# Early loads and an eleventh weight buffer for the experts, and their rows fetched one expert at a time

## What is computed

```
logits = h @ router                      # 256 x 8
top_logit, top_e = top_k(logits, 2)
gate = softmax(top_logit)
for expert e, over the rows routed to it:
    y = (silu(rows @ wg[e]) * (rows @ wu[e])) @ wd[e]     # wg, wu: 1024 x 3584, wd: 3584 x 1024
out = sum of the two gated y of each token
```

## Time and profile before

| | us |
|---|---|
| median of 3 runs | 2739.91 (2738.45 to 2746.37) |
| the profiled execution | 2743.33 |
| its span in the trace | 2741.4 |
| PE busy | 2639.1 (96%) |
| VectorE busy | 1197.7 (44%) |
| ScalarE busy | 442.7 (16%) |
| GpSimd (POOL) busy | 108.2 (4%) |

### The profile page before, as it was taken

The page is one execution under the profiler, slowest core; times in us unless marked ns, Lnnn a source line. Parts: engine busy times, 40 slices in busy tenths (PEclk is TensorE's granted clock), DMA queues, the critical chain, the costliest instruction groups (busy, mean ns, idle before and its releaser), DMA issues.

```text
span 2741.4 us, 48517 instructions
## 1 busy us (share of the span) xinstructions
PE 2639.1 (96%) x20537; PEld 1656.5 (60%) x20537; DVE 1197.7 (44%) x2895; ACT 442.7 (16%) x1054; POOL 108.2 (4%) x154
## 2 busy tenths in 40 slices
PE   8899999989899999999999998999979999999998
PEld 7659984865333233232332386699458967876993
DVE  3855675474110110110110166467655665344675
ACT  1231000133011010110110113200041001132000
POOL 1000000000100000000000011000000000050001
PEclk9999999999999999999999999999999999999999
DMA  7556555855999999999999946245504554232552
GB/s 224 175 182 206 169 170 183 269 167 197 338 418 419 417 416 411 410 419 406 408 420 410 413 153 108 70 154 170 172 14 154 170 172 135 77 85 70 169 170 93
DMA packets 234112, 642.91 MB, mean 235 GB/s; under 512 B 15673, under 2 KB 149185, under 8 KB 203056
## 3 DMA queue, kind: packets, MB, share of 16 engines
q1 hardware_dynamic: 225968, 616.89, 60.8%
q0 software_dynamic: 7264, 21.56, 3.5%
q10 hardware_dynamic: 672, 1.41, 0.1%
HBM read 626.73 MB, written 13.08 MB: 233 GB/s over the span
## 4 chain that ended last, share of the span: by engine, by line
PE 89%; DVE 6%; DMA 2%; issue 1%; POOL 1%; ACT 0%; DVEq 0%; ACTq 0%; POOLq 0%
PE pacc L1194 14%; PE pacc L1268 10%; PE pt L961 10%; PE pacc L1285 7%; PE pt L1268 7%; PE pt L1194 6%; PE pacc L1232 6%; PE pada L1294 4%; PE po L1268 3%; PE pacc L1135 3%; PE pt L1232 3%; PE pt L1173 2%; PE pt L1680 2%; PE pacc L1115 2%; PE po L1232 1%; DVE prob L2187 1%
## 5 line engine op out<-in xcount | busy, mean ns | idle before, releaser
L2527 DVE TENSOR_TENSOR gateb<-kT,pt 128x512 f32<-128x512 f32 (+1 forms) x32 | 19.9, 621 | 534.5 <-PE pt L1268 533.8
L1268 PE MATMUL pacc<-ring,bigc 128*32 128x512 f32 (+1 forms) x1920 | 188.3, 550 | 1.1 <-DVEq L2518 1.1
L961 PE MATMUL pt<-ring,hT 128*128 128x256 f32 x832 | 184.4, 381 | 0.0
L961 PEld LDWEIGHTS pt<-ring,hT 128*128 128x128 f32 x832 | 156.9, 190 | 25.6 <-issue 5.2
L1194 PE MATMUL pacc<-probT,prob 128*128 128x128 f32 x1440 | 170.6, 275 | 0.0
L1194 PEld LDWEIGHTS pacc<-probT,prob 128*128 128x128 f32 x1440 | 165.6, 192 | 0.0
L1285 PE MATMUL pacc<-ring,bigc 128*32 128x512 f32 x1280 | 151.2, 592 | 0.0
L1268 PE MATMUL pt<-ring,bigc 128*32 128x512 f32 (+1 forms) x1280 | 140.7, 560 | 8.2 <-DMA ring<-in_moe_w_up 8.2
L1232 PE MATMUL pacc<-prob,chunks 128*128 128x512 f32 x282 | 136.4, 592 | 0.0
L1268 PEld LDWEIGHTS pacc<-ring,bigc 128*32 128x32 f32 x1920 | 58.8, 110 | 127.2 <-issue 124.9
L2313 DVE TENSOR_TENSOR prob<-ring 128x512 f32<-128x512 f32 x86 | 59.5, 692 | 154.8 <-PE pacc L1194 108.5
(11 more groups left out here) (463 smaller groups left out, 4280.9 us busy)
## 6 DMA issues: line engine op xcount, KB each, us to landing
ring<-in_moe_w_down SPq DMA_DIRECT2D x80, 1024.0 KB, 17.5
ring<-in_w_gate_up SPq DMA_DIRECT2D x66, 1024.0 KB, 5.1
ring<-in_w_ada SPq DMA_DIRECT2D x48, 1024.0 KB, 5.3
ring<-in_moe_w_gate SPq DMA_DIRECT2D x48, 1024.0 KB, 8.5
ring<-in_moe_w_up SPq DMA_DIRECT2D x48, 1024.0 KB, 19.5
ring<-in_w_down SPq DMA_DIRECT2D x33, 1024.0 KB, 4.9
ring<-in_moe_w_gate SPq DMA_DIRECT2D x32, 768.0 KB, 15.0
ring<-in_moe_w_up SPq DMA_DIRECT2D x32, 768.0 KB, 12.8
```

What stands on the lines that cost most here:

```text
L961: ins = pe.matmul(t[:, q * 256:q * 256 + n], src[:, k, q * P:q * P + P], w[:, k, 0:n], start=(k == 0), stop=(k == KC - 1))
L1268: ins = pe.matmul(into[32 * j:32 * j + 32, 0:w].rearrange("p (t n) -> p t n", n=2 * 32), hcurv[:, kc, 32 * g:32 * g + 32], strip_columns(t ...
```

## The change

Three edits go together.

- `MOE_SLOTS` goes from 10 to 11; the eleventh buffer is columns 4096 to 6144 of `big`. The places are dealt anew: tile m with m % 11 = i below 6 goes to ring buffer (`pre_moe` + i - 2) % 6, the others to `xc`, the two halves of `prob`, `biasb` and the new one.
- Tiles 6, 9 and 10 of expert 0 are loaded by SP between the last `w_out` tile and the last six `w_ada` tiles. The other tiles of expert 0 below 11 are then loaded in the order 2, 3, 7, 4, 0, 1, 5, 8, and from tile 11 on, and for the experts 1 to 7, in order of m as before.
- POOL fetches the rows of one expert at a time from `slot_rows` straight into `next_slots`: those of expert 1 after the scatter, those of e + 2 when the sums of expert e are handed over. The copy on VectorE goes away with the array in `big`.

Semaphores are merged (`picked` into `routed`, `slots_arranged` and `y_shifted` into `rows_turned`), and the dense branch, which no longer has that part of `big`, uses other columns and waits for the fetches at its end.

```diff
-MOE_SLOTS = 10
+MOE_SLOTS = 11
+MOE_EARLY = (6, 9, 10)
+MOE_FIRST = (2, 3, 7, 4, 0, 1, 5, 8)
...
             i = m % MOE_SLOTS
-            return (pre_moe + i) % SLOTS if i < SLOTS else i
+            return (pre_moe + i - 2) % SLOTS if i < SLOTS else (6, 8, 9, 7, 10)[i - SLOTS]
...
-                   [xc[:, :], biasb[:, :], prob[:, 0:2048], prob[:, 2048:4096]]
+                   [xc[:, :], biasb[:, :], prob[:, 0:2048], prob[:, 2048:4096], big[:, 4096:6144]]
...
+            def load_expert(e, m, early=False):
...
+                i = moe_place(m)
+                if not early:
+                    sp.wait_ge(slot_free[i], e * moe_uses[i] + (m // MOE_SLOTS + 1))
+                sp.dma_start(moe_view(tile), src).then_inc(tile_loaded[i], 16)
...
                     load(n, item[1], item[2])
                     n += 1
+                    if n == pre_moe - MODS_ROUTER:
+                        sp.wait_ge(conv_taken, 2)
+                        sp.wait_ge(conv_ready, 2)
+                        for m in MOE_EARLY:
+                            load_expert(0, m, early=True)
...
-                    with sp.Fori(0, NE) as e:
-                        for m, tile in enumerate(moe_tiles):
...
+                    for m in MOE_FIRST + tuple(range(MOE_SLOTS, len(moe_tiles))):
+                        load_expert(0, m)
+                    with sp.Fori(1, NE) as e:
+                        for m in range(len(moe_tiles)):
+                            load_expert(e, m)
...
             pool.sem_inc(slot_free[7], 1)
+            pool.sem_inc(slot_free[10], 1)
...
-            for j in range(STRIPS):
-                pool.dma_start(slots_in[32 * j:32 * j + 32, 1:NE, :].rearrange("p e (g n) -> p (e g) n", g=3),
-                               slot_rows[CAP:NE * CAP, 256 * j:256 * j + 256].rearrange("(g t) n -> t g n", t=32))\
-                    .then_inc(slots_loaded, 16)
+
+            def fetch_slots(e):
+
+                for j in range(STRIPS):
+                    pool.dma_start(next_slots[32 * j:32 * j + 32, :].rearrange("p (g n) -> p g n", g=3),
+                                   slot_rows[e * CAP:e * CAP + CAP, 256 * j:256 * j + 256]
+                                   .rearrange("(g t) n -> t g n", t=32)).then_inc(slots_loaded, 16)
+
+            fetch_slots(1)
...
                     pool.dma_start(expert_rows[o + 32 * g:o + 32 * g + 32, 512:1024],
                                    ysum[64 * (g - 1):64 * (g - 1) + 32, 1, :]).then_inc(y_written, 16)
+                if e + 2 < NE:
+                    fetch_slots(e + 2)
                 pool.wait_ge(y_written, 64 * (e + 1))
                 pool.sem_inc(y_free, 1)
...
-                        ve.wait_ge(slots_loaded, 16 * STRIPS)
-                        ve.tensor_copy(next_slots, big[:, bass.ds((e + 1) * EW, EW)]).then_inc(slots_arranged, 1)
-                        ve.wait_ge(slots_arranged, e * 2 + 1)
+                        ve.wait_ge(slots_loaded, e * (16 * STRIPS) + 16 * STRIPS)
                         arrange(next_slots)
-                        weigh(e * 2 + 2)
-                    add_rest(e)
+                        weigh(e * 3 + 1)
+                    add_rest(e, last)
```

More of the change, by code:

```diff
@@ L333, in build @@
         y_copied = sem("y_copied")
-        y_shifted = sem("y_shifted")
         y_ready = sem("y_ready")
@@ L747, in load @@
                 sp.dma_start(slot_view(n, kind), src).then_inc(tile_loaded[n % SLOTS], 16)
+            gate_rows_of = W["moe_w_gate"][0].rearrange("e k f -> (e k) f")
+            up_rows_of = W["moe_w_up"][0].rearrange("e k f -> (e k) f")
+            down_rows_of = W["moe_w_down"][0].rearrange("e f n -> (e f) n")
+            def load_expert(e, m, early=False):
+                tile = moe_tiles[m]
+                kind, half, c, _ = tile
+                if kind == "d":
+                    src = down_rows_of[bass.ds(e * FF1 + 2 * P * c, 2 * P), :].rearrange("(p k) n -> p k n", k=2)
+                else:
+                    f0 = HALVES[half][0]
+                    src = (gate_rows_of if kind == "g" else up_rows_of)[bass.ds(e * D + P * c, P), f0:f0 + moe_width(tile)]
+                i = moe_place(m)
+                if not early:
+                    sp.wait_ge(slot_free[i], e * moe_uses[i] + (m // MOE_SLOTS + 1))
+                sp.dma_start(moe_view(tile), src).then_inc(tile_loaded[i], 16)
             for item in stream:
@@ L1308, in moe_sparse @@
             def moe_sparse():
-                pe.wait_ge(picked, 1)
+                pe.wait_ge(routed, 2)
                 for half in range(2):
@@ L2505, in arrange @@
                     ve.transpose(hcur.rearrange("p (b g t) -> p g b t", b=KC, t=32),
-                                 slots.rearrange("p (g b i) -> p g b i", b=KC, i=32)).then_inc(slots_arranged, 1)
+                                 slots.rearrange("p (g b i) -> p g b i", b=KC, i=32)).then_inc(rows_turned, 1)
                 def weigh(n):
-                    ve.wait_ge(slots_arranged, n)
+                    ve.wait_ge(rows_turned, n)
                     ve.tensor_tensor(hcurv, hcurv, free(g[:, 0:1], [[1, KC], [0, CAP]]), ALU.mult).then_inc(h_current, 1)
@@ L2536, in turn, with add_rest @@
                                  product[:, k % 2, 0:w].rearrange("p (t n k) -> p t k n", n=32, k=2)).then_inc(turned_taken, 1)
-                def add_rest(e):
+                def add_rest(e, last):
                     ve.wait_ge(y_done, e * 2 + 2)
@@ L2542, in add_rest @@
                     for g in range(2):
-                        ve.tensor_copy(yside[64 * g:64 * g + 32, :], down_rest[64 * g + 32:64 * g + 64, :]).then_inc(y_shifted, 1)
-                    ve.wait_ge(y_shifted, e * 2 + 2)
+                        ve.tensor_copy(yside[64 * g:64 * g + 32, :], down_rest[64 * g + 32:64 * g + 64, :]).then_inc(rows_turned, 1)
+                    ve.wait_ge(rows_turned, e * 3 + (2 if last else 3))
                     ve.tensor_tensor(ysum[0:96, 1, :], down_rest[0:96, :], yside[0:96, :], ALU.add).then_inc(y_ready, 1)
@@ L2630, in moe_dense @@
                 settle()
+                ve.wait_ge(slots_loaded, 16 * STRIPS * (NE - 1))
             def already(q):
@@ L2978, in _ @@
                         go(ve.tensor_scalar(pick[:, q, :], pick[:, q, :], den[:, 2 + q:3 + q], None, ALU.mult))
-                    tell(picked)
+                    tell(routed)
                     find_rows()
```

18 lines of the change are left out of this document (2 added, 16 removed).

## The result

The changed kernel takes 2812.99 us (median of 5 runs, 2809.25 to 2814.4), the kernel before 2738.45 (5 runs, 2734.53 to 2746.37): ratio 1.0266, 95% interval 1.0254 to 1.0279. Slower by 74.5 us, where 53.5 was forecast: 2793 us, in a range of 2768 to 2822. Run again on another chip it took 2809.78 against 2741.34, ratio 1.0245 (1.0228 to 1.0263). The profiled execution took 2812.99 us for a span of 2811.2.

The account below looks back on a forecast made before the run. PE was taken as the bound (busy 96% of the span), the DMA queues close behind; 49.3 + 16.2 + 1.5 - 13.5 = +53.5 us, giving 2796.8 for the profiled execution, 2793 for the median, range 2768 to 2822.

Parts of the forecast that it names:

- its rivals (2806 to 2835): Slower outcomes: clock falling at every boundary 0.14, thin queue with later landings 0.09, expert 0 keeping its stall 0.05.
- SP waits with tile 0 until tile 44 is used: Seven expert boundaries: tile 0 issued at E - 2.18, E being the next expert's stall-free start, after some 26 us idle.
- Tile 0 lands late by 3.1 us: Each boundary: tile 0, loaded into an empty queue, lands after 5.3 us, so PE stalls 3.1 us.
- Tile 1 stalls for 3.9 us: Each boundary: tile 1 is issued 1.2 us after tile 0's start, lands at E + 9.6, and stalls PE 3.9 us.
- Tiles 2 to 10 follow without a stall: Each boundary: these tiles land 2.50 us apart and are used at 2.58, so no more stall, but no lead.
- the first term of the sum: Landing stalls for tiles 0 and 1: 7.0 us per boundary, 49.3 us for seven.
- The six fetches cost 16.2 in full: Row fetches just after the boundaries of experts 0 to 5 delay weights 2.7 us each, 16.2 us; low end nothing.
- Rival: the clock on top, 20.3: PE's clock falls after the stalls at every boundary, 7 x 2.9 = 20.3 us more, about 2814; chance 0.14.
- Expert 0 saves 13.5: Expert 0's stall and slow clock both go, -13.5 us; either half alone leaves at most a 3 us stall.
- The end, +1.5: End of the experts' stage: the context load into `xc` lands later against the end, +1.5 us (-1 to +3).
- Before the stage, nothing: Three early tiles loaded before the w_ada tiles cost nothing, PE's need being covered by 20 us and more.
- 3 us to spare per expert: Per expert the queues need 105.1 us for weights and PE 108.2, so PE sets the pace with 3 us spare.

Follow-up runs that it names:

- the version without the fetches: The changed kernel without the row fetches of experts 2 to 7, which compute with expert 1's rows: 2801.41 us, ratio 1.0231 to the kernel before.
- the fillers: The changed kernel plus matmuls on a constant at the seven boundaries, three before the wait for tile 0, four before tile 1: 2803.05 us, ratio 1.0237.
- The rows alone: The kernel before with only the row fetches made one expert at a time, no early tiles, ten buffers: 2744.8 us, ratio 1.0014.
- the two early tiles alone: The kernel before with only tiles 6 and 7 of expert 0 loaded early, ten buffers, one big row fetch: 2732.85 us, ratio 0.9979.
- the version with both changes: The changed kernel with filler matmuls before tiles 0 and 1 and without the row fetches of experts 2 to 7: 2793.06 us, ratio 1.0201.
- the spread dealing: The changed kernel, eleven buffers, none reused within nine tiles, early tiles 0, 5, 11: 2735.11 us; also without row fetches of experts 2 to 7: 2729.34 us.

## Why the prediction was right

The mechanism came as forecast, and 2812.99 us is in the range. But it is 20 us above the 2793 of the sum, in the band that the prediction gave to its rivals (2806 to 2835), and two errors in the sum work against each other. By its steps:

- *SP waits with tile 0 until tile 44 is used.* Right: issued at E - 2.38 (forecast E - 2.18), after a gap of 25.9 us (some 26), with 0 GB/s before it.
- *Tile 0 lands late by 3.1 us.* Right: 3.05 to 3.33. A tile issued into the empty queue was in use after 818.50 - 813.00 = 5.5 us; the forecast had 5.3. The formula that the prediction quotes from the Trainium skill (DMA: Bandwidth & Descriptors, Anatomy of one DMA) is given there for DMAs issued by GpSimd; its 4.4 us for a tile of SP's is 1.1 under this row.
- *Tile 1 stalls for 3.9 us.* Right where the clock is full during tile 0: at the second boundary of the version without the fetches it was issued 1.19 us after tile 0's start (forecast 1.2; 932.38 against 931.19) and in use 5.0 later, a stall of 3.6. In the change the first one is issued at 820.56, 2.06 behind the start, at a slow clock, and in use 6.3 later, beside the rows; over the seven boundaries the pause is 3.1 to 4.4. The waits sum to 49.3 us, the very number of the forecast, but partly by luck: they are not the whole price.
- *Tiles 2 to 10 follow without a stall.* Wrong, and with it the first term of the sum was too small. Without the fetches the boundaries cost 71.0 us, not 49.3. Of the 21.7 us more, the fillers take away 11.5: that is slow clock, which the forecast left to a rival. The other 10.2 stay at full clock, where a boundary costs 59.5 / 7 = 8.5 us, not 7.0: at the second one, from start to start, 3.4 for tile 0, 3.8 for tile 1, and 0.5 and 1.1 for small pauses at tiles 2 and 8. At each of the seven, two tiles land 3.2 to 4.0 us apart where the others land 2.5 apart, and each time a 16 KB packet of the instruction queue lies between the two landings or 1 us before (the lines stand below the list); in the stage such a packet comes every 8 to 24 us; whether it is the cause was not tested.
- *The six fetches cost 16.2 in full.* Too large. Taking them out of the change saves 5.0 us at the boundaries. The 16.3 of the versions with fillers is no confirmation of the price of 2.7: it is 1.9 each at the four boundaries with the clock held, and 4.2 each at the two where it was not. The landing times give 1.5. The Trainium skill (DMA: Bandwidth & Descriptors, Issuing engines are not separate DMA queues) says that transfers of all issuing engines interleave on the same 16 DMA engines; the traces agree: with POOL's fetch SP's tile 1 came 7.82 us behind tile 0 at the second boundary with fillers, without it 6.35.
- *Rival: the clock on top, 20.3.* The fall itself came as described, 0.50 behind tile 1, but its price is smaller. Without the fetches it is 11.5, or 1.6 a boundary, where 2.9 was said. With them it is 0.9 at each of the four boundaries where the fillers held the clock, and the fillers' loss at the first and sixth leaves 0.2 in all. So that the time came out at this rival's 2814 is luck. The Trainium skill (TensorE: Matmul & The Clock Gate, HAM oscillation) advises to arrange the loop so that the engine is not left cold by waits for DMA; here the clock fell as it says, and fillers that held it at 1.00 at five of seven boundaries moved the stage by 1.0 us in 943.
- *Expert 0 saves 13.5.* 13.3. (Of the 5.3 us that the prediction puts to the clock there, its two slow tiles show 1.9 and 2.9.) The rows alone do all of it, the two early tiles alone 5.8 of it (115.86); a stall of 3.0 and one of 2.6 remained there, where 3 at most was said for either half.
- *The end, +1.5.* +2.3.
- *Before the stage, nothing.* +6.3 and +6.9 in the two profiles of the change; not foreseen, and the cause is open, as above.

The packets of the weights (q1) and the one of the instruction queue (q8) from 1063 to 1065 us in the version with both changes, between two landings at 1062.05 and 1066.08:

```profile
q1 hardware_dynamic: 115, 0.82, 98.5%
q8 instruction: 1, 0.02, 3.2%
```

In sum, 2796.8 was forecast for the profiled execution, and the difference to 2812.99 is 10.5 (boundaries: 21.7 too little for the tiles, 11.2 too much for the fetches) + 6.3 (before the stage) + 0.8 (end) + 0.2 (expert 0) - 1.6 (the rest) = 16.2 us.

One more step was wrong and did not show in the sum: "3 us to spare per expert". It took the 419 GB/s of a single window of 62 us for the rate of the whole stage. The kernel before gains at most 1.1 us per expert, and the spread dealing without the fetches none. By the forecast's numbers the change with harmless dealing would have given 2726. It gives 2740.49 with ten buffers and 2735.11 with eleven: what expert 0 wins by the smaller fetches, the later experts pay back.

## What to carry to other kernels

When N tiles go round M buffers and the issuer takes them in order, look at the seam: at N mod M = 2 the first tile of the next round waits for the last but one of this round, and all prefetch is gone, though there is one buffer more; deal the buffers by distance of reuse and check the seam tile by tile. Filling the queue with other tiles first makes it worse, since the urgent one then lands behind them. And where the queue's share is 1.0, its GB/s do not tell whether it has time to spare, since they may be the consumer's pace: follow the landing time of one tile from round to round. A transfer moved from a busy stretch to a "free" one comes back as time as soon as the lead is used up.

## What was not expected of the hardware

Two costs at the boundaries, the slow clock (11.5 us alone) and the small fetches (16.3 us alone), came to 16.5 together. And 384 KB of rows in pieces of 1 KB cost 1.5 us of a full queue (landing times) that moves such an amount of weights in 0.9 (393,216 bytes at 419 GB/s).
